# Kernel of a GLA and a Gated-DeltaNet layer: the second scan's coefficients stored in pieces, and its buffers laid out anew

## The reference

```
proj = h @ w_in ; q, k, v = silu(conv(qkv)) ; z, beta, log_a from proj
g = cumsum(log_a) ; decay = exp(g_i - g_j) for j <= i
m = strict_tril((k * beta) @ k.T * decay)           # per head and chunk, 64 x 64
u, w = solve(I + m, [v * beta, k * beta * exp(g)])
a_qk = (q @ k.T) * decay
for each chunk:                                     # 16 meta tokens, then 16 chunks of 64
    v_new = u - w @ s
    o = (q * exp(g)) @ s + a_qk @ v_new
    s = s * exp(g_last) + (k * exp(g_last - g)).T @ v_new
out = h + (rms_norm(o) * silu(z)) @ w_out
```

## Time and profile before

| | us |
|---|---|
| median of 3 runs | 1465.19 |
| the three runs | 1463.52 to 1466.24 |
| the profiled execution, its time | 1463.95 |
| the profiled execution, its span | 1462.2 |
| TensorE busy in it | 1425.5 |
| mean granted clock of TensorE | 0.996 of full |

### The profile page before, as it was taken

The page is one execution under the profiler, slowest core; times in us unless marked ns, Lnnn a source line. Parts: engine busy times, 40 slices in busy tenths (PEclk is TensorE's granted clock), DMA queues, the critical chain, the costliest instruction groups (busy, mean ns, idle before and its releaser), DMA issues.

```text
span 1462.2 us, 21408 instructions
## 1 busy us (share of the span) xinstructions
PE 1425.5 (97%) x8458; PEld 1198.3 (82%) x8458; DVE 762.5 (52%) x937; ACT 461.6 (32%) x957; POOL 419.0 (29%) x358
## 2 busy tenths in 40 slices
PE   7999999999999999999999999999989999999997
PEld 5777799978888888999999999978867767777776
DVE  5223622234444356645645698789944654444442
ACT  4332731133222243333344533421232631111121
POOL 3212043442101121212211167243442441222210
PEclk9999999999999999999999999999999999999999
DMA  5521244476444224444454222336368895555530
GB/s 193 175 87 36 80 131 147 146 254 209 158 159 163 75 58 116 128 107 111 112 155 160 84 80 74 92 92 178 115 210 231 247 233 146 148 148 159 166 87 29
DMA packets 213918, 200.35 MB, mean 137 GB/s; under 512 B 62873, under 2 KB 177065, under 8 KB 213570
## 3 DMA queue, kind: packets, MB, share of 16 engines
q1 hardware_dynamic: 207234, 187.53, 43.0%
q10 hardware_dynamic: 6592, 11.54, 2.9%
HBM read 131.93 MB, written 67.09 MB: 136 GB/s over the span
## 4 chain that ended last, share of the span: by engine, by line
PE 53%; DVE 6%; ACT 2%; DMA 2%; issue 1%; SPq 1%; DVEq 0%; POOLq 0%; ACTq 0%; POOL 0%
PE banks L2157 17%; PE banks L2955 12%; PE banks L2224 12%; DVE gdn L2476 4%; PE banks L2051 2%; PE banks L3044 2%; PE banks L3011 2%; PE banks L3016 2%; PE banks L2075 1%; PE banks L3025 1%; DMA gdn<-gdn_v 1%; PE banks L2999 1%; DMA gdn_z<-gdn 1%; PE banks L2968 1%; ACT gdn L2302 1%
## 5 line engine op out<-in xcount | busy, mean ns | idle before, releaser
L2157 PE MATMUL banks<-hn_hi,gdn 128*128 128x352 f32 x1488 | 300.5, 327 | 0.0
L2157 PEld LDWEIGHTS banks<-hn_hi,gdn 128*128 128x128 f32 x1488 | 242.1, 188 | 4.8 <-issue 3.1
L2476 DVE SCALAR_TENSOR_TENSOR gdn<-gdn,conv_taps,gdn 128x1040 f32<-128x1040 f32 x96 | 175.9, 1832 | 13.6 <-ACT gdn L2288 10.8
L882 PE MATMUL banks<-gdn,hn_hi 128*128 128x512 f32 x528 | 168.1, 400 | 4.0 <-POOL gdn L604 3.1
L2224 PE MATMUL banks<-gdn,hn_hi 128*128 128x512 f32 x512 | 163.8, 400 | 1.8 <-ACT gdn L2423 1.4
L2428 POOL TENSOR_TENSOR gdn<-gdn,gdn 128x1024 fp32r<-128x1024 f32 x31 | 87.1, 2810 | 270.3 <-ACT gdn L2263 270.3
L2157 PE MATMUL banks<-hn_lo,gdn 128*128 128x352 f32 x744 | 158.2, 321 | 0.0
L2157 PEld LDWEIGHTS banks<-hn_lo,gdn 128*128 128x128 f32 x744 | 125.6, 188 | 0.0
L882 PEld LDWEIGHTS banks<-gdn,hn_hi 128*128 128x128 f32 x528 | 99.2, 190 | 28.8 <-ACT gdn L434 3.9
L2224 PEld LDWEIGHTS banks<-gdn,hn_hi 128*128 128x128 f32 x512 | 96.2, 190 | 29.1 <-issue 3.1
L882 PE MATMUL banks<-gdn,hn_lo 128*128 128x512 f32 x264 | 104.5, 396 | 0.0
(11 more groups left out here) (315 smaller groups left out, 2286.4 us busy)
## 6 DMA issues: line engine op xcount, KB each, us to landing
gdn<-in_gdn_w_in SPq DMA_DIRECT2D x32, 512.0 KB, 4.1
gdn<-in_x SPq DMA_DIRECT2D x16, 512.0 KB, 4.1
gdn<-in_gla_w_in SPq DMA_DIRECT2D x32, 256.0 KB, 4.7
gdn_kq<-gdn SPq DMA_DIRECT2D x16, 512.0 KB, 3.8
gdn_v<-gdn SPq DMA_DIRECT2D x16, 512.0 KB, 3.5
gdn<-in_gdn_w_in SPq DMA_DIRECT2D x32, 256.0 KB, 4.8
gdn<-gdn_kq SPq DMA_DIRECT2D x16, 512.0 KB, 3.7
gdn<-gdn_ek SPq DMA_DIRECT2D x16, 512.0 KB, 5.8
```

Source lines behind the costliest of these rows:

```text
L882: mm = pe.matmul(out_bank(g, u, i), h_[:, kt, k], piece_of(w_, q), start=(kt == 0 and e == 0), stop=(kt == KT - 1 and e == 2))
L2157: last = pe.matmul(a[:, b, 0:m], w[n % 2][:, kt, :], x[:, kt, PAD + s:PAD + s + m], start=(kt == 0 and e == 0), stop=(kt == KT - 1 and e = ...
L2476: dve.scalar_tensor_tensor(cv[:, :], xs[:, tap:tap + L], T.cw[:, tap, t:t + 1], cv[:, :], ALU.mult, ALU.add).then_inc(S("ni_conv"), 1)
```

## The change

The meta tokens' `m_rows` is weighed by a function of its own, before the last part of the inverse, stored alone and loaded back at once. Of `sc`, two DMAs of 8 rows each (chunks 0 and 1 of all heads) go first; after the loads of the meta tokens' values and keys, eight DMAs of 14 rows each (chunks 2 to 15 of one head) store the rest. `load_ua(0)` and `load_ek(1)` wait for the first two alone and are issued ahead of the keys of chunks 0 and 1, which wait for all ten. The buffers are laid out so that `vn`, `St`, `ua` and `h[1]` lie behind the stored rows of `sc`. ScalarE waits for all ten before its first write of `h[0]`, in chunk 0.

```diff
@@ -1899,7 +1899,7 @@
                 return NQK + head_of_k(n) * P
             return 2 * NQK + v_of(n) * P
 
-        def sync(sp, ahead):
+        def sync(sp, ahead, meta_ahead):
             def load(n):
                 wait(sp, S("ni_whi"), n - 3)
                 wait(sp, S("ni_wlo"), n - 3)
@@ -2033,9 +2033,28 @@
                     sp.wait_ge(S("ni_ek_out"), 16 * NH)
                     ahead(sp)
             sp.wait_ge(S("ni_dec_in"), 16 + 16 * NH)
-            sp.wait_ge(S("ni_u"), 4)
+            sp.wait_ge(S("ni_u"), 1)
             sp.dma_start(T.gdn_uam, m_rows).then_inc(S("ni_uam_out"), 16)
-            sp.dma_start(T.gdn_ua, sc[:, 0:2 * C * C].rearrange("p (j x) -> p j x", x=2 * C)).then_inc(S("ni_ua_out"), 16)
+            sp.wait_ge(S("ni_uam_out"), 16)
+            meta_ahead(sp)
+            sp.wait_ge(S("ni_u"), 3)
+            for c in range(2):
+                sp.dma_start(T.gdn_ua.rearrange("(g c) j x -> c g (j x)", c=NCH)[c], sc[c::NCH, 0:2 * C * C])                  .then_inc(S("ni_uam_out"), 16)
+
+        def store_ua(sp):
+
+            for h in range(NH):
+                rows = slice(h * NCH + 2, (h + 1) * NCH)
+                sp.dma_start(T.gdn_ua[rows], sc[rows, 0:2 * C * C].rearrange("p (j x) -> p j x", x=2 * C))                  .then_inc(S("ni_ua_out"), 16)
+
+        def ua_first(eng):
+
+            eng.wait_ge(S("ni_uam_out"), 48)
+
+        def ua_stored(eng):
+
+            eng.wait_ge(S("ni_uam_out"), 48)
+            eng.wait_ge(S("ni_ua_out"), 16 * NH)
 
         def store_z(sp, k):
             sp.wait_ge(S("ni_zev"), k + 1)
@@ -2623,9 +2642,12 @@
                 for r, c in ((slice(0, 32), slice(0, C)), (slice(32, C), slice(32, C))):
                     dve.tensor_tensor(sc_rows[:, r, 0, c], sc_rows[:, r, 0, c],
                                       bc(beta[:, r, :], [P, 32, c.stop - c.start]), ALU.mult).then_inc(S("ni_u"), 1)
+
+            def weigh_meta():
+
                 dve.wait_ge(S("ni_minv"), steps(NMETA))
                 dve.tensor_tensor(m_rows, m_rows, bc(m_g[:, 1, :].rearrange("p (j o) -> p j o", o=1),
-                                                     [NH, NMETA, NMETA]), ALU.mult).then_inc(S("ni_u"), 2)
+                                                     [NH, NMETA, NMETA]), ALU.mult).then_inc(S("ni_u"), 1)
 
             def steps(size):
 
@@ -2679,10 +2701,12 @@
             ev_v(NV // P - 2, 2)
             ev_v(NV // P - 1, 0)
             ev_v(NV // P - 1, 2)
+            weigh_meta()
             for _ in inverse:
                 pass
             weigh()
         F.sync, F.tensor, F.scalar, F.gpsimd, F.vector = sync, tensor, scalar, gpsimd, vector
+        F.store_ua, F.ua_first, F.ua_stored = store_ua, ua_first, ua_stored
         F.store_z, F.z_stored, F.z_out, F.z_last_group, F.tiles = store_z, z_stored, z_out, z_last_group, G3 * TT
     return F
 
@@ -2722,17 +2746,20 @@
         ss2, ssl = sums[:, 0:1], sums[:, 1:2]
         assert ahead.end <= FRONT
         behind.end = ahead.end
-        St = behind.take([P, NH, NDV])
         oT_hi = behind.take([P, KO, P], F32R)
         oT_lo = behind.take([P, KO, P], F32R)
-        kq_at, ek_at, St_at = 0, 2 * NH * 2 * C, ahead.end
+        og = [behind.take([P, HP, NDV]) for n in range(2)]
+        h0 = behind.take([P, D])
+        kt = [behind.take([P, HP, NDK]) for n in range(2)]
+        assert behind.end <= FRONT + 2 * C * C
+        behind.end = FRONT + 2 * C * C
+        vn = behind.take([P, HP, NDV])
+        kq_at, ek_at, St_at = 0, 2 * NH * 2 * C, behind.end
+        St = behind.take([P, NH, NDV])
+        ua = [behind.take([P, HP, 2, C]) for n in range(2)]
+        h = [h0, behind.take([P, D])]
         last_hi = A.at(St_at, [P, KO, P], F32R)
         last_lo = [A.at(n, [P, KO // 2, P], F32R) for n in (kq_at, ek_at)]
-        og = [behind.take([P, HP, NDV]) for n in range(2)]
-        vn = behind.take([P, HP, NDV])
-        kt = [behind.take([P, HP, NDK]) for n in range(2)]
-        ua = [behind.take([P, HP, 2, C]) for n in range(2)]
-        h = [behind.take([P, D]) for n in range(2)]
         junk = T.hn_hi_f32[:, :, D:TP]
         nw = T.hn_lo_f32[:, :, D:TP]
         EARLY = 2
@@ -2799,6 +2826,12 @@
                          bc(T.gdn_ek[0:1].rearrange("c h x -> c (h x)"), [P, NH * 2 * C])).then_inc(S("ns_in_ek"), 16)
             tokens(sp, v, T.gdn_v, NMETA, C, R, S("ns_in_v"))
             sp.dma_start(hnw[:, :], head_norm).then_inc(S("ns_in_hnw"), 16)
+
+        def sync_meta(sp):
+
+            for p in range(2):
+                sp.dma_start(um[RM[p], :, :], T.gdn_uam.rearrange("(h p) j i -> p j h i", p=2)[p])\
+                  .then_inc(S("ns_in_m"), 16)
 
         def sync(sp):
             def load_kq(m):
@@ -2848,9 +2881,6 @@
                 load_h(t + 2)
 
             def load_meta():
-                for p in range(2):
-                    sp.dma_start(um[RM[p], :, :], T.gdn_uam.rearrange("(h p) j i -> p j h i", p=2)[p])\
-                      .then_inc(S("ns_in_m"), 16)
                 tokens(sp, vm, T.gdn_v, 0, NMETA, RM, S("ns_in_m"))
                 keys(ktm, 0, NMETA, RM, S("ns_in_m"))
 
@@ -2894,13 +2924,14 @@
                     store_out((m - 5) // 2)
                 if m % 2 == 0 and m >= 6:
                     next_h((m - 6) // 2)
-            sp.wait_ge(S("ni_uam_out"), 16)
             load_meta()
+            F.store_ua(sp)
+            F.ua_first(sp)
+            load_ua(0)
+            load_ek(1)
+            F.ua_stored(sp)
             load_kt(0)
             load_kt(1)
-            sp.wait_ge(S("ni_ua_out"), 16)
-            load_ua(0)
-            load_ek(1)
             for n in range(2):
                 sp.wait_ge(S(("ni_zhi", "ni_zlo")[n]), KT * F.tiles // TT + 4)
             load_rows(0, 1)
@@ -3138,6 +3169,8 @@
                 wait(act, S("ns_ss"), HP * m)
                 wait(act, S("ns_ss2"), t - 1)
                 wait(act, S("ns_og"), HP * m)
+                if m == 0:
+                    F.ua_stored(act)
                 scrap = h[0][:, :].rearrange("p (a b) -> p a b", b=P) if m < 2 else junk
                 for hp in range(HP):
                     act.activation(scrap[:, 2 * hp:2 * hp + 2, :], pQ[:, hp, :].rearrange("p (a b) -> p a b", b=P),
@@ -3145,7 +3178,7 @@
                 others(m, 2)
                 if j and m < NCH - 1:
                     high(m - 1)
-            act.wait_ge(S("ni_ua_out"), 16)
+            act.wait_ge(S("ni_u"), 3)
             act.wait_ge(S("ns_mv"), 1)
             act.activation(vn[RM[0], :, :], pK[RM[0], :, :], ACT.Copy).then_inc(S("ns_mvn"), 1)
             act.wait_ge(S("ns_in_hnw"), 16)
@@ -3233,7 +3266,7 @@
                     residual(t - 1, 1)
                 if j and m < NCH - 1:
                     lo(m - 1)
-            dve.wait_ge(S("ni_ua_out"), 16)
+            dve.wait_ge(S("ni_u"), 3)
             dve.wait_ge(S("ns_mv"), 1)
             dve.tensor_copy(vn[RM[1], :, :], pK[RM[1], :, :]).then_inc(S("ns_mvn"), 1)
             for rnd in range(2):
@@ -3312,6 +3345,7 @@
             pool.tensor_scalar(ss2[:, :], ss2[:, :], 1.0 / D, ssl[:, 0:1], ALU.mult, ALU.add).then_inc(S("ns_rs2"), 1)
             pool.wait_ge(S("ns_rs2"), 2 * TT)
             pool.tensor_tensor(ss2[:, :], ss2[:, :], T.minus_half[:, 0:1], ALU.pow).then_inc(S("ns_rs2"), 1)
+        B.meta_ahead = sync_meta
         B.ahead, B.sync, B.tensor, B.scalar, B.gpsimd, B.vector = sync_ahead, sync, tensor, scalar, gpsimd, vector
     return B
 
@@ -3324,7 +3358,7 @@
 
         @block.sync
         def _(sp):
-            F.sync(sp, B.ahead)
+            F.sync(sp, B.ahead, B.meta_ahead)
             B.sync(sp)
 
         @block.tensor
```

## The result

The changed kernel takes 1480.08 us (median of 4 runs, 1478.03 to 1483.53) against 1464.36 (1461.34 to 1466.24, 4 runs of the kernel before on the same chip): ratio 1.0112, 95% interval 1.0084 to 1.014. It is slower, by 16 us where 36 were forecast and inside the range of 1464 to 1510.

A forecast was written before the change was run, and what follows sets the result against it. TensorE (PE), 97% busy, bounds the kernel, with stops at the z slots behind the coefficients' store. Rows ending +34 us later plus +2 for what waits gave +36: 1463.95 to 1500 us, range 1464 to 1510.

The forecast's parts named there:

- the cause and the sign: Coefficients' store: eight DMAs of 14 neighbouring rows run slowly and make the kernel slower; slower by more had chance 0.81.
- meta coefficients ahead, 0: SyncE between 1057.1 and 1074.66 us: storing and loading the meta coefficients early costs 0 and gains 0.
- new places, 0: Buffers moved behind the rows: engines no longer wait for the store before the meta part, worth 0.
- the inverse ends sooner, 1 us: VectorE: with `weigh_meta` early, `weigh` ends near 1073.6 instead of 1074.6, gaining SyncE 1 us.
- first two chunks apart: Two 8-row stores ahead of the rest: 2.5 us from below, twice that if two rows share one way.
- the rest, 39.7 us: Eight DMAs of 14 rows: 8 x 4.96 us, range 9.9 to 61, last row near 1120 instead of 1086.2.
- The factor of 4: Time per row packet in the eight stores: four times the undisturbed one, since 16-partition stores looked four times slower.
- the part-sharing rival: Eight stores: engines drift apart, fewer rows share a way; two sharing 19.8 us, kernel 1479; three, 1489; chance 0.13.
- its three-row case, 29.8 us: Eight stores, three rows sharing one way into the memory: 29.8 us for the rows, kernel 1489.
- What waits for it. The z stores, first.: ScalarE's z slots: tile 17's store stuck behind rows, PE stops near 1087, meta product 9 to 10 us after rows, +2.
- they keep their distance ... so they add nothing: SyncE's later keys, z loads, `w_out` rows and chunk 1's values: PE moves as much as they do, so 0.
- the clock: PE after the z stop: low clock already lost some 3 us before; six matmuls at low clock counted 2.6 us.

The follow-up runs named there:

- x5: The kernel before with one edit: the coefficients' store as eight DMAs of 16 neighbouring rows, none of the new order or places: 1481.85 us, ratio 1.0115.
- x4: The changed kernel without the first two chunks apart, all 128 rows stored by eight DMAs of 16 rows 8 apart: 1472.83 us, ratio 1.0056.
- x3: The changed kernel without the first two chunks apart, all 128 rows stored by eight DMAs of 16 neighbouring rows: 1483.97 us, ratio 1.0131.
- x12: The kernel before with `weigh_meta` early and the meta tokens' coefficients stored and loaded ahead; old store, places and waits kept: 1463.58 us, ratio 1.0003.
- x15: x1_one measured once more, in more rounds: 1462.36 us, ratio 1.0001.
- x6: The changed kernel with its two small stores kept, the rest stored by one DMA of 128 rows into a second buffer: 1470.44 us, ratio 1.0042.
- x11: x6 with the one DMA of 128 rows issued right behind the two small stores, ahead of the meta loads: 1471.45 us, ratio 1.0058.
- x13: The changed kernel, first chunk's coefficients loaded sooner and SyncE waiting for z stores of tiles 18 to 22 before the eight stores: 1477.89 us, ratio 1.0106.
- x7: x6, first chunk's coefficients loaded sooner and SyncE waiting for z stores of tiles 18 to 22 before the 128-row DMA: 1470.94 us, ratio 1.0038.
- x9: x7 with the second chunk's coefficients and values issued ahead of SyncE's wait for the 128-row DMA: 1465.21 us, ratio 1.001.
- x8: The changed kernel with the load of the second chunk's values put ahead of that chunk's coefficients: 1477.49 us, ratio 1.0095.
- x14: The changed kernel with the second chunk's coefficients and values issued ahead of SyncE's wait for the eight stores: 1480.6 us, ratio 1.0124.
- x1_one: The changed kernel with the first two chunks no longer apart and all 128 rows stored by one DMA: 1460.38 us, ratio 0.9974.

## Why the prediction was right or wrong

*Right: the cause and the sign.* The form of the rest decides: x5 gives a loss as large from it alone. That rows share a way out of the memory is shown for the small stores (2.50 us for 1.25) and by x4 against x3, which differ in the rows' distance alone (26.8 us for 32.1); that it is the whole of the loss is not, see x3 and x4 above.

*Right: meta coefficients ahead, 0; new places, 0.* x12 and x15 are the kernel before to within 0.2%, and x5 against x3 (1481.85, 1483.97, intervals overlapping) says the same beside a slow store.

*Not borne out, and small: the inverse ends sooner, 1 us.* `weigh_meta` took 0.40 us at 953, but the two operations of `weigh` took 4.52 us (3.43 before), and the release came at 1074.5, not 1073.6.

*Right at its upper bound: first two chunks apart.* 2.5 us for each store, 5 in all, from the half of the range where two rows share. What the step left small was the loads behind them: SyncE was held 5.49 us in two, so the rest began at 1082.9 and not between 1077.2 and 1080. The forecast had no separate price for this step; with a good form behind it, it is 6 to 8.5 us (x6, x11).

*Mis-sized: the rest, 39.7 us.* It is 29.6 (x13). The row took 2.6 us and not 4.96. The factor of 4 came from two stores of 8 and 32 KB whose difference of 0.3 us is a printed tenth either side; its own bound of 120 GB/s was the right end, 124 measured. A row took about twice its undisturbed time, as if two rows and not four shared a way, the first case of the part-sharing rival (19.8 us). That the length is nevertheless that of its three-row case, 29.8 us, goes with the engines having had no row for 31% of the time (69.2% in the queue's share from 1088 to 1104), a term that the sum did not have. How the rows of two stores overlap can't be seen, since the profile's rows don't part the engines. The Trainium skill's 104 GB/s for 16 rows (SBUF — State Buffer, Door 1) would give an estimated 35 us; here the measurement decides, and it lies above that rate in x3_near too (130). With the later start the rows ended near 1082.9 + 29.6 = 1112.5 by this estimate, where 1120 was forecast; in the trace itself the last row begins between 1113.5 and 1114. This is worth at most 7.5 of the missing 18.6 us.

*Failed: "What waits for it. The z stores, first."* The step had SyncE's rings (what is issued and waits at the DMA engines) full of rows until the end, z packets one to a row, and tile 17's store therefore late by 30 us. In fact SyncE's issue was held 3.3 us in each small store. At the ends of the third to the eighth issue 22 to 34 rows had been issued and not begun, about two stores' worth and not everything that was left, and 13 z packets went by for each row. z tiles 21, 22 and 23 passed; only 24 and 25 stopped, and 25 went at 1101.0, 11 us before the rows were done. The meta product came at 1101.68, +7.6 us, where 1130 was forecast (1094.06 + 36). x7, x9 and x13, which take the rows away from the z stores and lose the stop with them, show that this is the place; that the held issue is the reason why the stop was short is read from the rows of SyncE's queue, and was not tried by itself. Why engines had no row while two stores' rows were issued stays open.

*Failed: "they keep their distance ... so they add nothing".* The step tied PE to the end of the rows. Since PE was released 11 us before it, everything issued behind SyncE's wait became late relative to PE: values of chunk 1 +6.2 us. x8, x14 and x13 move this stop to chunk 3, to chunk 0's keys, and to 16 us of keys, while x5, whose PE was held until SyncE had issued the keys behind the rows, has no such stop. It reads as one debt: the rows occupy 30 us, and PE pays at whichever point it first needs what stands behind them.

*Left out: the clock.* Some 3 us of low clock were counted as existing already. After 13.07 us of standstill PE ran 14.7 us instead of 11.1 to chunk 0, +3.6, and the stop in chunk 1 cost more of the same kind within the 6.2. The +3.6 belongs to this one execution: x3, x4, x5 and x14 took 10.4 to 11.3 us there behind stops of 13.7 to 15.5. So 3.6 of the +17.4 is chance as much as change.

*The sum.* +9.4 at the slots, +3.6 clock, +6.2 late loads, -1.8 by the scatter ahead of the first mark: +17.4 in the profiled spans, against +34 and +2. The part-sharing rival gave 1479 and 1489 and met the number with the first, by luck, for its sum was another: its rows ended at 1099.7 and PE followed them, while here they ended near 1112.5 and PE did not wait for the last.

## What to carry to other kernels

Leave a large store whole, or split it by columns, which here made the store 4 us longer and cost the kernel nothing. In DMAs of 16 rows the same bytes ran at a third of the rate (130 GB/s for 359), with the rows apart at less than half (156), and the issuing engine was held. Before a large transfer is moved or delayed, list what stands behind it on its queue and what shares its engines: here the orders that removed the stop at the z slots put another behind it, which took back all of the gain (x7) or a good part of it (x9, x13). And compare executions by marks inside the trace: a stretch of the same work took 8, 11 or 14 us by the clock alone, which is more than the change that x1_one seemed to show.

## What the runs showed of the hardware that was not expected

- Issuing a DMA is not free when other DMAs are waiting: 3.3 us (median) for each store of 14 neighbouring rows on SyncE, 4.13 us for one z store on ScalarE, 0.42 us for the one of 128 rows. On ScalarE this delayed the weight splits behind it, and PE waited 5.2 us for GpSimd in x3_near.
- Stores of 4.19 MB took 11.7 us as 128 rows, 15.5 in columns, 26.8 for rows 8 apart and 32.1 for neighbouring rows.
- Eight 32 KB rows on partitions 16 apart took 2.50 us each, in a store over all partitions 1.25.
- z packets of 1 KB: one to a row of 32 KB beside the store of 128 rows, 13 to a row beside the stores of 14.
- The profiled executions reach the same z store, which comes ahead of the rows, at times from 1070.5 to 1075.7 us. The same kernel gave 1070.97 and 1072.20 (x1, x15). What makes this scatter stays open.
